# Running all stages in front of the experts twice, for 240 and for 320 columns, with expert items among the stages of the second run

## The reference, cut to what matters

```python
xn  = rmsnorm(h); p = xn @ w_in            # 2048 -> 8208 columns, split among 8 GDN and 8 FoX heads
# GDN head: conv of width 4 + silu on q|k|v, l2-normed q and k, gated delta rule in exact chunks:
u   = triangular_solve(strict_lower(beta * decay * k k^T), beta * (v - eG * (k S)))
o   = eG * (q S) + (q k^T * decay) u;  S = eG_last * S + (k * tail)^T u
# FoX head: softmax attention with a forget bias; the samples also read 256 past rows out of a paged cache
h   = h + concat(gdn, fox) @ w_out
# PEER: for each token and each of 8 heads the 16 best of 128*128 experts:
hid = gelu(xi . expert_u[idx]);  y = sum((gate * hid) * expert_v[idx])
```

## Time and profile before

| | us |
|---|---|
| median of 3 runs | 5341.08 (5330.65 to 5343.3) |
| the profiled execution | 5321.39 |
| its span | 5319.7 |
| last GDN head's write to `mixT` | 1091.1 |
| last FoX head's write to `mixT` | 1980.1 |
| tile 0 routed | 2188.8 |
| all tiles routed | 3543.3 |

### The profile page before, as it was taken

One profiled execution on the slowest core, in us unless ns is written; L12 is line 12 of the kernel. 1 busy time (PEld: TensorE's weight loads), 2 busy tenths in 40 slices (PEclk: granted clock), 3 DMA queues, 4 the chain that ended last, 5 costly groups with the idle time before them and its releaser, 6 DMA issues. The chain is left out here.

```text
span 5319.7 us, 35009 instructions
## 1 busy us (share of the span) xinstructions
PE 2322.2 (44%) x12099; PEld 1829.1 (34%) x12099; DVE 3336.2 (63%) x3914; ACT 440.2 (8%) x844; POOL 2715.0 (51%) x1556
## 2 busy tenths in 40 slices
PE   6999989779999977484604203000000000000000
PEld 5777777667777766473302101000000000000000
DVE  2344343411111112576899999989889998899897
ACT  1122221211211110000000000000000000000000
POOL 1121122122243220164566566658888878888786
PEclk7999999989999978796756556555555555555555
DMA  3121111031222116698999989889999999999998
GB/s 96 32 63 45 44 41 41 9 88 52 61 79 67 52 51 206 216 372 321 336 357 379 362 360 367 358 329 418 406 413 420 420 401 420 413 420 420 394 420 324
DMA packets 420533, 1339.91 MB, mean 252 GB/s; under 512 B 31860, under 2 KB 270912, under 8 KB 277312
## 3 DMA queue, kind: packets, MB, share of 16 engines
q0 software_dynamic: 171136, 1177.91, 54.9%
q1 hardware_dynamic: 249296, 160.80, 10.8%
HBM read 1314.72 MB, written 23.85 MB: 252 GB/s over the span
## 5 line engine op out<-in xcount | busy, mean ns | idle before, releaser
L1510 DVE SCALAR_TENSOR_TENSOR ex_y<-ex_ring,ex_wt,ex_y 128x2048 f32<-128x2048 f32 x539 | 1266.2, 2349 | 86.5 <-DMA ex_ring<-in_peer_v_dram,idx_all 72.3
L1497 DVE CUSTOM_DVE_ANT_0 ex_ring<-ex_ring,ex_xi 128x2048 f32<-128x2048 f32 x544 | 1243.8, 2288 | 81.8 <-DMA ex_ring<-in_peer_u_dram,idx_all 32.3
L1444 POOL DMA_INDIRECT ex_ring<-in_peer_v_dram,idx_all x512 | 1055.8, 2062 | 369.9 <-DVE ex_hid L1497 217.8
L1444 POOL DMA_INDIRECT ex_ring<-in_peer_u_dram,idx_all x512 | 1033.5, 2019 | 412.3 <-DVE ex_y L1510 179.3
L449 PE MATMUL fox_pj<-xnT,fox_w 128*128 128x256 f32 (+1 forms) x2048 | 557.1, 430 | 18.1 <-DMA fox_w<-in_w_in_dram 18.1
L449 PE MATMUL gdn_pj<-xnT,gdn_w 128*128 128x256 f32 (+1 forms) x2048 | 529.8, 408 | 21.6 <-DMA gdn_w<-in_w_in_dram 11.5
L449 PEld LDWEIGHTS fox_pj<-xnT,fox_w 128*128 128x128 f32 x2048 | 411.4, 206 | 111.3 <-DMA fox_w<-in_w_in_dram 18.2
L449 PEld LDWEIGHTS gdn_pj<-xnT,gdn_w 128*128 128x128 f32 x2048 | 383.4, 195 | 97.9 <-DMA gdn_w<-in_w_in_dram 11.8
L1310 POOL DMA_INDIRECT fox_kc<-in_cache_k_dram,fox_idx x128 | 123.5, 965 | 480.4 <-DVE fox_idxf L1238 443.8
L1758 PE MATMUL route_b_ps<-skT,route_b_q 128*128 128x128 f32 (+1 forms) x128 | 32.2, 415 | 611.2 <-ACT route_b_q L1771 611.2
L1758 PEld LDWEIGHTS route_b_ps<-skT,route_b_q 128*128 128x128 f32 (+1 forms) x128 | 23.2, 264 | 622.3 <-ACT route_b_q L1771 615.9
(11 more groups left out here) (398 smaller groups left out, 3452.4 us busy)
## 6 DMA issues: line engine op xcount, KB each, us to landing
gdn_w<-in_w_in_dram SPq DMA_DIRECT2D x32, 1024.0 KB, 7.3
fox_w<-in_w_in_dram SPq DMA_DIRECT2D x32, 1024.0 KB, 6.4
out_a_w<-in_w_out_dram SPq DMA_DIRECT2D x8, 2048.0 KB, 9.0
route_a_w<-in_peer_w_query_dram SPq DMA_DIRECT2D x16, 1024.0 KB, 6.0
out_b_w<-in_w_out_dram SPq DMA_DIRECT2D x8, 2048.0 KB, 31.2
route_b_w<-in_peer_w_query_dram SPq DMA_DIRECT2D x16, 1024.0 KB, 20.5
ex_ring<-in_peer_u_dram,idx_all POOLq DMA_INDIRECT x512, 13.3
ex_ring<-in_peer_v_dram,idx_all POOLq DMA_INDIRECT x512, 13.2
```

Source lines behind the costliest of these rows:

```text
L1444: pool.indirect_dma_start(self.ring[:, i % RING, :], None, self.tables[which], bass.IndirectOffsetOnAxis(ap=self.index(s, g, k), axis=0)). ...
L1497: nc.vector.tensor_tensor_reduce(ring, ring, self.xi[:], 1.0, 0.0, ALU.mult, ALU.add, self.hid[:, g % 2, k:k + 1]).then_inc(self.sem["cons ...
L1510: nc.vector.scalar_tensor_tensor(y, ring, wt, y, ALU.mult, ALU.add).then_inc(self.sem["consumed"], 1)
```

## The change

All stages from the norm to the routing become one function, `front`, which runs twice. `FIRST` holds 240 columns in two tiles (112 rows: 32 sample, 16 meta and 64 prompt rows; and 128), `LATER` the other 320 in three (128, 128, 64). `w_in`, `w_out` and `w_query` are read in both runs. The GDN state and the last three columns ahead of the convolution stay in SBUF between the runs; keys and values of the first run go to DRAM and come back. The second run has the expert items of the first among all its stages: `OVERLAP` gives 12, 144, 144, 48, 8 and 48 items to norm, GDN, FoX, `mix_out`, `ffn_norm` and `route`, 404 in all. A GDN head has 12 places for them (1.5 items each), a FoX head 8 (2.25 each). 684 items are left for the end. The prompt's 64-row tiles are folded in two. The ring has 6 buffers. Inside a GDN head, the mask of a level moves from GpSimd to VectorE (it masks `QT` as it takes it out of PSUM), some column scalings move to ScalarE, and the loops over heads are written out.

```diff
-OVERLAP = (64, 16, 336)
-RING = 7
+FIRST = Group("a", 0, (0, 112, 240), 0)
+LATER = Group("b", 240, (0, 128, 256, 320), 2)
+NONE = {"norm": 0, "gdn": 0, "fox": 0, "out": 0, "ffn": 0, "route": 0}
+OVERLAP = {"norm": 12, "gdn": 144, "fox": 144, "out": 48, "ffn": 8, "route": 48}
+RING = 6
...
-            norm_and_gates(nc, ins, outs, mem, scr)
-            gdn_heads(nc, ins, outs, mem)
-            fox_heads(nc, ins, outs, mem, scr)
-        token_rows(nc, ins, outs, mem, scr, Group("a", FIRST), None, (0, 0, 0))
+            front(nc, ins, outs, mem, scr, FIRST, None, NONE)
...
-        token_rows(nc, ins, outs, mem, scr, Group("b", LATER), stream, OVERLAP)
+        front(nc, ins, outs, mem, scr, LATER, stream, OVERLAP)
...
+def front(nc, ins, outs, mem, scr, group, stream, quotas):
+    with ExitStack() as tokens:
+        mem["mixT"] = tokens.enter_context(nc.sbuf_tensor(f"mixT_{group.tag}", [P, KT, group.cols], F32))
+        with ExitStack() as heads:
+            mem["xnT"] = heads.enter_context(nc.sbuf_tensor(f"xnT_{group.tag}", [P, KT, group.cols], F32))
+            norm_and_gates(nc, ins, outs, mem, scr, group, stream, quotas["norm"])
+            gdn_heads(nc, ins, outs, mem, group, stream, quotas["gdn"])
+            fox_heads(nc, ins, outs, mem, scr, group, stream, quotas["fox"])
+        with ExitStack() as rows:
+            mem["hres"] = rows.enter_context(nc.sbuf_tensor(f"hres_{group.tag}", [P, group.n, D], F32))
+            mix_out(nc, ins, mem, group, stream, quotas["out"])
+            mem["xiT"] = mem["mixT"]
+            ffn_norm(nc, ins, outs, mem, scr, group, stream, quotas["ffn"])
+        route(nc, ins, mem, group, stream, quotas["route"])
...
+                if samples:
+                    sp.wait_ge(sem["turn_done"], h + 1)
+                    sp.dma_start(B.state[:], ins["state_gdn"][0, :, h].rearrange("b k v -> k b v")).then_inc(sem["state_in"], 16)
...
                 for l in range(1, LV + 1):
+                    dve.wait_ge(sem["QT_done"], h * LV + l)
+                    nc.vector.tensor_tensor(B.QT[:], tiles(R1), cst("levels", l * P, (l + 1) * P).unsqueeze(1)
+                                            .to_broadcast([P, T, P]), ALU.mult).then_inc(sem["QT_masked"], 1)
+                    share.take(dve, next(points))
                     dve.wait_ge(sem["YT_done"], h * LV + l)
+                    nc.vector.tensor_tensor(wide(B.XT), wide(B.XT), R1[:, 0:TW], ALU.subtract).then_inc(sem["XT_ready"], 1)
```

More of the change, by code:

```diff
@@ L75, in constant_parts @@
         "after": np.concatenate(after, 1),
-        "levels": np.concatenate(levels, 1),
+        "not_upto": np.concatenate([np.where(m, 0.0, NEG) for m in upto[:2]], 1),
+        "not_after": np.concatenate([np.where(m, 0.0, NEG) for m in after[:2]], 1),
+        "levels": np.concatenate(levels[:1] + [m.T for m in levels[1:]], 1),
         "ident": row == col,
@@ L87, in constant_parts @@
         "row": row,
-        "fold": (row % NS == np.arange(NS)[None, :]),
     }
@@ new lines, in attend @@
+                pe.wait_ge(sem["gU_ready"], n)
+                if samples:
+                    for t in range(T):
+                        nc.tensor.matmul(R2[:, t * P:(t + 1) * P], tcst("after", t), B.gU[:, t, :], start=True, stop=False)
+                        last = nc.tensor.matmul(R2[:, t * P:(t + 1) * P], ident, tcst("not_upto", t), start=False, stop=True)
+                else:
+                    nc.tensor.matmul(R2[:, 0:TW], tcst("after", 0), wide(B.gU), start=True, stop=False)
+                    last = nc.tensor.matmul(tiles(R2), ident, mask("not_upto"), start=False, stop=True)
@@ L767, in _ @@
-            head(HEADS - 1, True)
+                attend(h, h + 1 == HEADS)
+            share.gelu(act, share.steps)
         @block.vector
@@ new lines, in attend, with sampled @@
+                scores(1)
+                scores(2)
+                for i in range(1, T + 1):
+                    outputs(i)
+                    if i + 2 <= T:
+                        scores(i + 2)
+                ahead.take(4)
+                pe.wait_ge(sem["oN_ready"], n)
+                for t, (a, b) in enumerate(group.tiles):
+                    last = nc.tensor.transpose(R2[:, a:b], B.oN[0:b - a, t, :], ident[0:b - a, 0:b - a])
+                last.then_inc(sem["oT_done"], 1)
+            def sampled(h, ahead):
+                n = h + 1
+                ident, ones = cst("ident"), cst("ones")
@@ L1156, in _, with stored @@
-            with pe.Fori(0, HEADS - 1) as h:
-                head(h, Ahead(h + 1, AHEAD, nc, pe, sem, B.w, pj, xnT))
-            head(HEADS - 1, Ahead(None, AHEAD))
         @block.scalar
         def _(act):
-            for r in range(2):
-                act.sem_inc(sem[f"evacuated{r}"], 1)
+            def stored(own, h):
+                if h > 0 and samples:
+                    for name in (f"{own}_out0", f"{own}_out1", f"{own}s_out"):
+                        act.wait_ge(sem[name], 16 * h)
+                if h > 0:
+                    act.wait_ge(sem[f"{own}_kept"], 32 * h)
@@ L1218, in _ @@
+            for h in range(HEADS):
                 attend(h)
+            share.gelu(act, share.steps)
         @block.vector
@@ L1348, in token_rows @@
-def token_rows(nc, ins, outs, mem, scr, group, stream, quotas):
-    with ExitStack() as rows:
-        mem["hres"] = rows.enter_context(nc.sbuf_tensor(f"hres_{group.tag}", [P, group.n, D], F32))
-        mix_out(nc, ins, mem, group, stream, quotas[0])
-        mem["xiT"] = mem["mixT"]
-        ffn_norm(nc, ins, outs, mem, scr, group, stream, quotas[1])
-    route(nc, ins, mem, group, stream, quotas[2])
+                for out, row, rows, own in ((kp, ks, B.kN, "k"), (vp, vs, B.vN, "v")):
+                    for t in range(T):
+                        own_rows, at = group.seq_rows(t)
+                        pool.dma_start(out[at, h, :], rows[own_rows, t, :]).then_inc(sem[f"{own}_out{t}"], 16)
+                    pool.dma_start(row[:, h, :], rows[0:NS, 0, :]).then_inc(sem[f"{own}s_out"], 16)
@@ new lines, in __init__ @@
+        self.sets, places = [], 0
+        for group, tiles in ((FIRST, (1, 0)), (LATER, (0, 1, 2))):
+            for t in tiles:
+                rows, at = group.prompt_rows(t)
+                parts = [(rows, y_prompt[at])] + ([(slice(0, NS), y_sample)] if group.samples and t == 0 else [])
+                for rows, y_rows in parts:
+                    fold = P // (rows.stop - rows.start)
+                    self.sets.append(self.Set(group, t, fold, rows, places, y_rows, self.sets[-1].end if self.sets else 0))
+                    places += TOPK * self.sets[-1].groups if fold > 1 else 0
@@ L1377, in __init__ @@
+        self.groups = self.sets[-1].end
+        self.items = 2 * TOPK * self.groups
         self.set_of = [s for s in self.sets for _ in range(s.groups)]
@@ L1727, in route @@
     share = Share(stream, quota, HEADS * PARTS)
-    first = group.tiles[0]
-    whole = sum(r == P for r in group.rows)
     with ctx:
```

1483 lines of the change are left out of this document (807 added, 676 removed).

## The result

The changed kernel took 5482.64 us (median of 4 runs, 5474.45 to 5490.24) against 5340.12 for the one before: a ratio of 1.027, 95% interval 1.025 to 1.0289. It is slower by 142 us, where the prediction said 5275 with a range of 5155 to 5435. The span of the profiled execution is 5481.2 us, against 5319.7: 161.5 more, since the profiled execution of before lay some 20 us under its median.

The account below looks back on a forecast made before the run. Stage latencies were taken to decide, with TensorE filling the heads and DMA the end. First run 1458 plus second run 2001 gave routing done at 3459; 1790 more made a 5249 span, written as median 5275, range 5155 to 5435.

Parts of the forecast that it names:

- GDN head, two tiles: ... = 66.5: First run without items: a GDN head falls from 118.7 to 66.5 us, eight of them 532.
- the term for the history, 5.5 us: First run's GDN head: the history load, behind one more weight load, comes later by up to 5.5 us.
- without items 118.7 − 26.1 − 5.5 ... = 64: Second run's GDN head, three tiles and no samples: 64 us before its 18 items are added, 89.5 with them.
- FoX head ... I take 67: Second run's FoX head with items beside projection and attention of three tiles: 67 us, between 52 and 105.
- rival D: Items at GDN and FoX places hide nothing: heads of 106 and 87 us, median 5567; chance 0.08.
- for kept keys on the first: Second run's FoX stage: 10 us added once, on the first head, making 546 for eight heads.
- The price of the items among the heads: Second run: 18 items take a GDN head from 64 to 89.5 us; a FoX head with items takes 67.
- C: Much faster: heads shrink with their columns, GDN 55 us for 66.5 and 83 for 89.5; 5085 in all; chance 0.15.
- Rival B: Second run: TensorE waits for items, its clock falls to 0.7 from 0.95, 160 us more, median 5435; chance 0.22.
- the main case: The summed forecast, range 5215 to 5335, chance 0.55, with clock over 0.8 in the second run's GDN.
- The rule of the Trainium skill: Products that wait repeatedly restart at half rate: second run's TensorE 61 us a GDN head become 122, about 5795; chance 0.03.
- or the chain didn't shorten: First run's GDN head: upper bound of 118.7 us if the chain did not shorten at all; lower bound 51.

Follow-up runs that it names:

- the bare one: The changed kernel with every OVERLAP quota 0, so no items beside the stages and all 1088 at the end: 5981.95 us, ratio 1.1218 to the kernel before.

## Why the prediction was wrong

The sign was wrong and the time outside the range. Point by point, by its own steps:

- **"GDN head, two tiles: ... = 66.5"** failed by 7.7. The step that failed first is the term for the history, 5.5 us. TensorE stood 7.2 us on average for it (in the kernel before, 1.4 us over seven heads), and some 2 more went to a lower rate behind the wait. With the history loaded first the head is 66.9, of which 2.0 are still a wait for it, so the other terms of that line, which together say 61, were 4 short as well.
- **"without items 118.7 − 26.1 − 5.5 ... = 64"** failed by 11.5, the largest error: 75.5. The level was right (3.56 us measured, 3.6 said), a link of the state chain too (2.70). What failed is to take off all of the 26.1 us of shorter projection and two links of the chain beside it, and 12 for the samples with the history in it. Of the 48 projection steps that stand ahead, the program puts two in each link of the state chain and leaves the rest for the start of the next head. With five links 5 are left there, with three 9. So that block did not shrink, first in the kernel before, then in the bare one:

```profile
382.19 6.24 PE L449 MATMUL gdn_pj<-xnT,gdn_w 128*128 128x256 f32 x20
```

```profile
1933.47 6.43 PE L505 MATMUL gdn_b_pj<-xnT_b,gdn_b_w 128*128 128x320 f32 x18
```

And a link takes 2.70 us though its two steps are shorter by 0.41 each. Counted that way the projection and the two links are worth some 25 us and not 31.4 (an estimate: 49 steps of the other places at 0.41 each, and 5.1 for the chain). The history had cost next to nothing, and the samples' passes come to 8.3 (from 475.5, the first product with their states, to 483.8, the first link of the chain), not 12. The two together are 10 of the 11.5.
- **"FoX head ... I take 67"** failed by 11.4. The bare head takes 58.8, near TensorE's own 53.5 of work in it; the prediction has a bare head only under rival D, at 45. The kept values cost 7.9 of waiting on top, 9.2 with what follows from it. The prediction gave them 10 us once, "for kept keys on the first"; TensorE waited for them in six of the seven heads of the window.
- **The price of the items among the heads** was too high: 25.5 us a GDN head were said and 20.1 came. For FoX 22 (67 less rival D's 45) stand against 19.6, but that is near by luck, since 9.2 of the 19.6 are the late values and the items alone cost 10.4. Rival D, items that hide nothing, is out, and so is C, heads in proportion to their columns, which wanted 55 us.
- **Rival B** had the sign but the wrong cause. The granted clock in the second run's GDN stage was 0.85, over the 0.8 that the main case asked for, and raising it to 0.90 changed no head there. The rule of the Trainium skill, "TensorE: Matmul & The Clock Gate", section "HAM oscillation — how this bites in real kernels", carried through, wanted 122 us a head. The trace disagrees for GDN of the second run, where TensorE waited again and again, up to 3.3 us in the levels: 0.85 with items against 0.92 without, and heads of 95.6 us. It agrees in kind on the waits for the history, up to 8.5 us: with them cut short, the granted clock of that stage is 0.93 in place of 0.88.
- **"or the chain didn't shorten"** was kept as a bound for one run, but the bounds of both runs were never added up. The sum of two bare heads against one, 149.6 against 118.7, is the number by which the change should have been judged.
- The end (1790, measured 1800.3), the routing, the products and the start were right, each within 11 us.

So the loss is: 398 us of head time paid twice, of which some 58 (8 x 7.3) are the late history; 37 us of other stages; 18 at the end; less 292 that the items give back beyond what they did before (an item cost 1.27 us in place of 1.95). The late values are no part of the 398, since the bare kernel does not wait for them; they are 68 us by which the items give back less than they could.

## What to carry to other kernels

Splitting a staged kernel into two runs pays twice for the part of each stage that does not depend on its size; measure that part first, by two splits or by running the stages bare, and set it against what the overlapped work gives back, item by item. Spread work by where the engine waits, not evenly: the same 18 items a head cost 1.12 us each at even places and 0.37 in the waits. After a loop is cut into shorter turns, read the queues again for small transfers that stand behind large ones: two of these cost 117 us here by the medians (49 and 68; by the ratios some 106), and reordering a few lines mended them.
